# Two free quarters behind the neighbourhood turnings, a final normalisation by half rows, and a rank released by its own products

## The reference

```python
y = token_mixing(x * (1 + scale1) + shift1, ...)      # mLSTM, neighbourhood attention, HGRN2, three gates
x = layer_norm(ALPHA * x + gate1 * y, ln_g[0], ln_b[0])
y = hier_moe(x * (1 + scale2) + shift2, ...)          # top 1 of 4 groups, then top 2 of its 4 experts
x = layer_norm(ALPHA * x + gate2 * y, ln_g[1], ln_b[1])
```

```python
s = concatenate([q @ k_loc + bias, q @ cache_k], -1)  # group 1: local keys and cached context keys
p = softmax(s); out = p_loc @ v_loc + p_ctx @ cache_v

def layer_norm(x, g, b):
    mu = mean(x, -1); var = mean(square(x - mu), -1)
    return (x - mu) * rsqrt(var + LN_EPS) * g + b
```

## Time and profile before

| | |
|---|---|
| median of 3 runs | 1446.16 us (1442.0 to 1446.17) |
| profiled execution, its own time | 1447.57 us |
| its span, from first to last instruction | 1445.7 us |
| PE busy | 1376.5 us, 95% of the span |
| DVE, ACT, POOL busy | 519.8, 234.3, 152.4 us |
| mean granted clock of PE | 0.986 of full speed |

### The profile page before, as it was taken

How to read it: one execution, slowest core, us unless ns; L and a number is a source line. 1 busy time by engine, 2 the same in 40 slices (tenths; PEclk the granted TensorE clock), 3 DMA queues, 4 the chain that set the end, 5 groups by cost and what they waited for, 6 DMA issues and landing times. The chain is left out here.

```text
span 1445.7 us, 16958 instructions
## 1 busy us (share of the span) xinstructions
PE 1376.5 (95%) x6664; PEld 719.1 (50%) x6664; DVE 519.8 (36%) x984; ACT 234.3 (16%) x436; POOL 152.4 (11%) x130
## 2 busy tenths in 40 slices
PE   6999999999999999999989999999999999999994
PEld 2445455444444655555534554554444465555552
DVE  1353444322134432322244443542412452322324
ACT  0131220222201111111012222112321111011110
POOL 0114240111200000000001242301220000000000
PEclk8999999999999999999999999999999999999998
DMA  9754544645458299999974445544446628999993
GB/s 384 317 214 155 221 190 168 237 170 212 192 202 342 83 396 401 408 413 412 386 292 158 180 180 203 191 147 180 189 153 250 274 89 362 405 404 404 403 413 137
DMA packets 40264, 379.93 MB, mean 263 GB/s; under 512 B 7946, under 2 KB 12170, under 8 KB 17292
## 3 DMA queue, kind: packets, MB, share of 16 engines
q1 hardware_dynamic: 31776, 375.83, 64.8%
q10 hardware_dynamic: 8428, 3.29, 0.9%
HBM read 374.76 MB, written 4.33 MB: 262 GB/s over the span
## 5 line engine op out<-in xcount | busy, mean ns | idle before, releaser
L936 PE MATMUL psum<-ring,hT 128*128 128x512 f32 x1152 | 520.6, 601 | 3.9 <-ACT hT L1132 2.2
L936 PEld LDWEIGHTS psum<-ring,hT 128*128 128x128 f32 x1152 | 213.9, 192 | 244.1 <-issue 238.1
L1042 PE MATMUL psum<-ring,tbuf 128*64 128x256 f32 x1920 | 216.0, 380 | 1.9 <-DMA ring<-in_stream 1.9
L1042 PEld LDWEIGHTS psum<-ring,tbuf 128*64 128x64 f32 x1920 | 136.0, 137 | 95.1 <-issue 18.8
L1081 PE MATMUL psum<-ring,tbuf 128*64 128x512 f32 x512 | 116.9, 598 | 1.9 <-ACT tbuf L1327 1.9
L1601 DVE TENSOR_TENSOR ch<-psum,bias_ring 128x512 f32<-128x512 f32 x68 | 47.0, 691 | 172.3 <-PE psum L936 165.7
L1737 DVE TENSOR_SCALAR tbuf<-tbuf 128x256 f32<-128x256 f32 x32 | 9.4, 295 | 242.2 <-ACT tbuf L1317 242.2
L960 PE MATMUL psum<-ring,tbuf 128*128 128x512 f32 x192 | 82.9, 593 | 0.0
L1892 POOL TENSOR_SCALAR ldata<-ldata 128x512 f32<-128x512 f32 x24 | 46.1, 1922 | 284.7 <-ACT ldata L1279 284.7
L1026 PE MATMUL psum<-tbuf,ch 128*128 128x128 f32 x512 | 66.6, 285 | 7.7 <-DVE tbuf L1732 5.0
L1838 POOL TENSOR_TENSOR tbuf<-const,sm 128x512 f32<-128x512 f32 x16 | 20.4, 1295 | 475.6 <-DVE sm L1481 448.7
(11 more groups left out here) (269 smaller groups left out, 1174.9 us busy)
## 6 DMA issues: line engine op xcount, KB each, us to landing
ring<-in_stream SPq DMA_DIRECT2D x158, 2048.0 KB, 9.3
ch<-in_stream SPq DMA_DIRECT2D x6, 2048.0 KB, 12.4
bias_ring<-in_b_in SPq DMA_DIRECT2D x36, 256.0 KB, 8.1
ldata<-in_ldata SPq DMA_DIRECT2D x2, 2329.0 KB, 23.9
hbuf<-in_ln SPq DMA_DIRECT2D x4, 1024.0 KB, 12.0
hbuf<-in_stream SPq DMA_DIRECT2D x1, 2048.0 KB, 8.3
tbuf<-in_stream SPq DMA_DIRECT2D x1, 2048.0 KB, 11.6
ch<-in_lb_logits SPq DMA_DIRECT2D x2, 1024.0 KB, 13.6
```

What stands on the lines that cost most here:

```text
L936: mm = pe.matmul(bank(PJ + g), hT[:, k, g * P:(g + 1) * P], w[:, k, :], start=(k == 0), stop=(k == KT - 1))
L1042: mm = pe.matmul(psum[halves_of[hf], UP[j], 0:FE // 2], xgT[:, k, halves_of[i]], w_up[:, k, hf * (FE // 2):(hf + 1) * (FE // 2)], start=(k ...
```

## The change

There are three parts.

1. Two entries in SPARE: one free quarter behind `na_turn` and `na_probs` of group 1.
2. The wait for the experts' last sums is taken out of `no_pass` and put into the new function `residual`, for each half row of each group, as far as that bank needs. `finish` is split into `residual` (per half row) and `normalise`. At the end of a layer the first half row of group 1 is done before group 0 is modulated for the next layer. The `hold_clock` at the layer's end has 3 products in place of 6.
3. `ranked` is released by the third counting product. The two for the whole write to the next bank and release a semaphore of their own, `totalled`, for which DVE waits where it needs the largest of them.

```diff
-SPARE = {..., ("gate", 0): 1, ("decay", 1): 1, "na_scores": 1}
+SPARE = {..., ("gate", 0): 1, ("decay", 1): 1, "na_scores": 1, ("na_turn", 1): 1, ("na_probs", 1): 1}
...
-                pe.matmul(psum[:, T, NE:2 * NE], rest[1], sent[:, 1, :], start=False, stop=True)
-                pe.matmul(psum[:, T, 2 * NE:3 * NE], ones, sent[:, 0, :], start=True, stop=False)
-                pe.matmul(psum[:, T, 2 * NE:3 * NE], ones, sent[:, 1, :], start=False, stop=True).then_inc(ranked, 1)
+                pe.matmul(psum[:, T, NE:2 * NE], rest[1], sent[:, 1, :], start=False, stop=True).then_inc(ranked, 1)
+                pe.matmul(psum[:, T + 1, 0:NE], ones, sent[:, 0, :], start=True, stop=False)
+                pe.matmul(psum[:, T + 1, 0:NE], ones, sent[:, 1, :], start=False, stop=True).then_inc(totalled, 1)
...
                 if l + 1 < DEPTH:
-                    hold_clock(6)
+                    hold_clock(3)
...
+                def residual(sub, g, hf):
...
+                    else:
+                        dve.wait_ge(spread, (l * PASSES + 1) * (NE * 4) + (2 * g + hf + 1))
+                        src = bank(Y_MOE[g][hf])
...
-                    link(dve.tensor_reduce(most, sums[:, G, :], X, ALU.max))
+                    dve.wait_ge(totalled, l + 1)
+                    link(dve.tensor_reduce(most, psum[:, T + 1, 0:NE], X, ALU.max))
...
-                    dve.wait_ge(spread, (l * PASSES + 1) * (NE * 4) + 4)
...
-                for g in range(G):
-                    finish(1, g)
-                    if l + 1 < DEPTH:
-                        modulate(l + 1, 0, g, 2 + 2 * g)
+                finish(1, 0)
+                residual(1, 1, 0)
+                if l + 1 < DEPTH:
+                    modulate(l + 1, 0, 0, 2)
+                residual(1, 1, 1)
+                normalise(1, 1)
+                if l + 1 < DEPTH:
+                    modulate(l + 1, 0, 1, 4)
```

More of the change, by code:

```diff
@@ L154, in ready_quarter @@
     return 4 * chunk + 2 * g + 2
-SPARE = {"prep": 2, "silu": 1, "state": 1, "norm_state": 2, "cumsum": 1, "max": 1, ("gate", 0): 1, ("decay", 1): 1, "na_scores": 1}
+SPARE = {"prep": 2, "silu": 1, "state": 1, "norm_state": 2, "cumsum": 1, "max": 1, ("gate", 0): 1, ("decay", 1): 1, "na_scores": 1, ("na_turn", 1): 1, ("na_probs", 1): 1}
 ROTATE_AT = 24
@@ L440, in build @@
         sent_ready = sem("sent_ready")
-        ranked = sem("ranked")
+        ranked, totalled = sem("ranked"), sem("totalled")
         fullest_ready = sem("fullest_ready")
@@ L1630, in _, with normalise @@
                                 tt(yh, yh, lnt, ALU.add).then_inc(br_added, 1)
[L1633 to L1642, removed]
-                        else:
[L1644 to L1651, removed]
+                def residual(sub, g, hf):
+                    if sub == 0:
+                        if g:
+                            dve.wait_ge(slot_used, used(l, AT[l]["out", l, hf]))
+                        else:
+                            dve.wait_ge(out_filled, l * 2 + (hf + 1))
+                        src = bank(2 * hf + g)
+                    else:
+                        dve.wait_ge(spread, (l * PASSES + 1) * (NE * 4) + (2 * g + hf + 1))
+                        src = bank(Y_MOE[g][hf])
+                    xh = x[:, g, hf * W:(hf + 1) * W]
+                    link(tt(lnt, src, gate_b[sub][:, 2 * hf + g, :], ALU.mult))
+                    if sub == 0:
+                        link(stt(out=xh, in0=xh, scalar=ALPHA, in1=lnt, op0=ALU.mult, op1=ALU.add))
+                    else:
+                        link(tt(xh, xh, lnt, ALU.add))
+                    link(dve.bn_stats(bn6[:, g, hf, :], xh), dve_tick)
+                def normalise(sub, g):
                     link(dve.bn_aggr(bn2[:, g, :], bn6[:, g, :, :].rearrange("p a b -> p (a b)")))
@@ L1657, in finish @@
                         .then_inc(x_ready, 1)
+                def finish(sub, g):
+                    dve.wait_ge(ln_loaded, l * 64 + (32 * sub + 32))
+                    for hf in range(2):
+                        residual(sub, g, hf)
+                    normalise(sub, g)
                 finish(0, 0)
@@ L1689, in _ @@
                 dve.wait_ge(ranked, l + 1)
-                sums = psum[:, T, 0:3 * NE].rearrange("p (a n) -> p a n", a=3)
+                sums = psum[:, T, 0:G * NE].rearrange("p (a n) -> p a n", a=G)
                 link(stt(out=rank, in0=sums[:, 0:G, :], scalar=1.0, in1=sent, op0=ALU.add, op1=ALU.mult))
```

## The result

The changed kernel takes 1433.63 us (median of five runs, 1432.91 to 1435.45), against 1446.16 for the kernel before (five runs, 1442.0 to 1447.72). The ratio is 0.9909, with a 95% interval of 0.989 to 0.9928. The forecast was 1434, thus 12 us less; measured are 12.5.

What follows compares the result with a forecast made beforehand. PE was taken as the bound, busy almost throughout, leaving its waits, low clock and DVE's tail: 7.2 + 3.4 + 1.0 + 1.7 + 0.9 = 14.2 us off 1447.57, plus half of 1.6, rounded to 1434; range 1430.5 to 1438.5.

Steps and rivals of the forecast that it cites:

- The six waits: PE's waits for ACT at `na_cache` and both `na_out`, 1.20 us each, would all go: 7.2 us.
- I cost all of this at nothing: Later bias, sigmoid and copies behind the two free quarters would not delay PE: 0 us; uncovered, up to 1.2 each.
- such a wait between chunks 13 and 17: Sign of being wrong: PE waiting for DVE or ACT in that stretch; no size given.
- The falls of the clock: Two stretches at 1.2 GHz behind layer 0's `na_out` would go once PE is fed: 3.4 us.
- a new place: Allowance for a clock fall striking where the profiled execution had none: half of 1.6 us added.
- The rank: At the first gather of each layer, DVE and the gather start 0.45 us earlier: 0.9 us in all.
- at once in two: Clock falls in the two gathers stay at one of two; bounds 0 and 1.6 us on either side.
- The end of the layer: DVE starts the last tail 1.0 us earlier; between the layers PE begins the projection 1.7 us earlier.
- One sum: Between the layers, three constant products begun at 732.76 end by about 737.1 even at 1.2 GHz.
- The sum: Whole kernel: 14.2 us off the profiled execution, less an allowance for new clock falls, giving 1434 us.
- The rival of the returning clock: Waits go, but two low-clock stretches fall into PE's remaining short waits: + 3.4 us, 1437.5; chance 0.20.
- The experts-by-loads rival: Loads pace the experts, so the earlier gather gains nothing: + 0.9 to 2 us, about 1435.5; chance 0.08.

Runs made afterwards that it cites:

- part 1 alone: Only the two new SPARE entries, added to the kernel before: 1438.86 us, ratio 0.9946.
- part 2 alone: Only the new end of the layer (split `finish`, DVE's order, three constants), on the kernel before, timed twice: 1446.4 us both times.
- part 3 alone: Only the earlier release of `ranked` by the third counting product, on the kernel before: 1442.91 us, ratio 0.9986.
- the changed kernel without part 3: The changed kernel with one semaphore behind all five counting products again: 1439.69 us, ratio 0.9939.

## Why the prediction was right, point by point

**The six waits** (7.2 us forecast) went. In layer 0 the stretch became 7.45 us shorter: three waits of 1.20, two falls of the clock of 1.70, and some 0.15 us more at each wait than its own length. In layer 1, which had no fall, it became 3.02 us shorter, where 3.6 was forecast; the new wait of 1.07 us is in it.

**"I cost all of this at nothing"** is the step that failed. I followed the copies and the bias through ACT, but not its empty round. `na_scores` now stands behind an even quarter, one quarter after `na_cache`. Its wait for round n-1 of ACT is released only behind the sigmoid: 1.07 us. In layer 0 the modulation's eight products (L718, 1.9 us) stand between quarter 55 and `na_cache`, and the sigmoid is over before PE comes to `na_scores`. In layer 1 nothing stands there. The prediction named such a wait between chunks 13 and 17 as what would prove it wrong, and it was there. So the time came within a microsecond of the forecast although this sign of being wrong was seen. It cost 1.07 us of 14.2 in this trace, and more in others: of the six traces that have it, three show a fall behind it, as in part 1 alone. Removing it and its twin in group 0 gave 3.6 +- 1.3.

**The falls of the clock** (3.4 us, less 0.8 for a new place). In this trace both falls at `na_out` and the one at the gather are gone, and one came where there had been none, behind the unchanged wait of `na_out` of group 0 in layer 1:

```profile
969.95 1.08 PE L868 MATMUL psum<-ch,tbuf 128*128 128x64 f32 x8 [1.59 <-issue]
970.86 5.35 PE L936 MATMUL psum<-ring,hT 128*128 128x512 f32 x8
```

So 5.1 us less and 1.7 more, 3.4 in all where the forecast had 2.6. The 3.4 us for `na_out` were read from one trace with two falls. The other three traces that have these four waits (part 2 alone twice, part 3 alone) have two, one and one. That is six falls at sixteen places, or 2.6 us an execution, and the new wait at L856 brings back about 0.9. Over all runs the mean granted clock says more than one trace: 0.9878 before and 0.9916 after. That is 0.0038 of 1446, 5.5 us, with the falls inside the constants of `hold_clock`, which cost less or nothing. But not all of it comes from where I put it. Part 1 alone has 0.9877, as before, and its trace has a fall behind the new wait and one at the second gather; the 1.7 us left of 2.6 less 0.9 are below the 0.0013 (1.9 us) to which this mean is known. Part 3 alone has 0.9894 and the changed kernel without part 3 has 0.9887. The clock's share was booked under part 1, and much of it belongs to the rank.

**The rank** (0.9 us forecast). The start is 0.45 us earlier each time, exactly. The chance of a fall I left "at once in two". The shorter wait brought none in any of the eight traces with part 3 (sixteen gathers). Of the twelve gathers without it, with a wait of 1.35 us, seven fell. So the term is 0.9 plus about half of 1.7 for each of two gathers, near 2.6 us, and the runs say 3.1 +- 1.2 alone and 4.7 +- 2.1 in company. This term was mis-sized. The upper bound given for it was 0.9 + 1.6 = 2.5.

**The end of the layer** (1.0 and 1.7 us forecast; 1.0 and 1.8 in the traces). The steps are in the trace as worked out: x ready, PE waiting for it, the half row ahead of `modulate`. One sum was wrong without harm: six records of at most 0.86 us from 732.76 on end by 737.9 and not by 737.1, but DVE is in its half row until 739.3 either way (at 1.2 GHz the three constants took 4.51 us). And the 1.7 us is what is won where the clock falls in the six constants, as in four of five traces; in the fifth it would be 0.2. In the time little of the 2.8 us is seen: 0.3 +- 1.1 alone, 1.7 +- 1.8 and -0.1 +- 2.3 in company (the last is the kernel without part 3 against part 1 alone). The traces hint where it goes. Four pairs of traces differ by part 2 alone, and in each layer 1 as a whole is longer with it: by 2.6 and 2.8 us on the kernel before, by 2.9 with part 1, by 0.7 with parts 1 and 3. In the nine traces with part 2, layer 1's experts took 247.8 us on average, in the five without it 247.1. The fall behind the 1.59 us in layer 1 struck in three of the nine and in none of the five. That would be 1.4 us given back. But all falls in layer 1 together are seven in the nine traces and three in the five, and the mean granted clock of the 24 runs is that of before (0.9877 and 0.9878), so more time at the low clock is not shown. In the experts PE does wait for loads, in all by 0.4 to 2.6 us, as here in the first trace of part 2 alone:

```profile
PE psum L1042 <- DMA ring<-in_stream: 2.6, 4, 0.9
```

Why an earlier start of layer 1 should bring this is open. Waits of this kind also came in traces without part 2, and fourteen traces are too few to call it shown.

**The sum** came out right in part by luck, because its errors cancel: part 2 gives less than was booked, part 1's falls were fewer than in the trace read, the new wait costs 1.1 us and falls of its own, and part 3 gives 2 us or more beyond its term. The rival of the returning clock is partly true. The experts-by-loads rival is not what decides: the 0.45 us won at each gather passes on. Less 1.6 us for each fall in a gather, layer 0's experts took 246.8 us on average in the eight traces with part 3 and 247.1 in the six without it, layer 1's 247.1 and 247.3: they are not longer for having begun earlier. By the Trainium skill, DMA: Bandwidth & Descriptors, "Where 436 GB/s comes from", about 358 GB/s from HBM per core binds, and the loads would have swallowed the 0.45 us. The traces and runs do not agree: the changed kernel moved up to 416 GB/s there, and part 3 alone was 3.1 +- 1.2 us faster.

## What to carry to other kernels

When a round is moved, look at every semaphore that it waits for, also those of engines with nothing to do in it: an empty round signals only behind the work queued ahead of it (1.07 us here). A wait of about a microsecond on PE can cost 1.7 us more than it lasts, so shortening or filling it may be worth more than its length. A gain that stands plainly in a trace's stage must still be looked for in the mean of many runs, with the edit taken out of the finished kernel and not only added to the old one.

## What was unexpected of the hardware

- The granted clock was at half (1.2 GHz) for 3.4 us at a time after waits of only 1.1 to 1.6 us beside short products, and which wait brought it changed from one execution to the next. Each cost about 1.7 us (5.35 instead of 3.65 for a quarter). With the wait at 0.34 us it did not come at the four `na_out` of the one trace that has it; with 0.90 us at the gather, never in sixteen.
- The kernel before spread over 12.7 us in 63 executions, about as much as the whole change brings. The start, up to `na_turn` in layer 0, varied from 295.0 to 298.1 us in the twelve traces in which its code is unchanged.
- After the branch behind the experts in layer 0, PE stood for 2.3 to 2.8 us before its first product in all fourteen traces. What fills this time is not shown.
